# First norm from token rows in two channel halves, and expert outputs gathered by place, in a decoder step on one Trainium2 core

## The reference, cut to what matters

```python
def modulate(x, g, shift, scale):
    return rmsnorm(x, g) * (1 + scale) + shift
# per layer; the six parts are silu(c) @ ada_w + ada_b, 9 rows (prompt, 8 samples)
sh1, sc1, gt1, sh2, sc2, gt2 = adaln_params(c, ada_w[l], ada_b[l])
h = modulate(x, norm1_g[l], sh1, sc1)
z = h @ w_in[l]                       # 1536 columns: u | v | p
...                                   # gated chunk mixer and pooling mixer
x = x + gt1 * mix
h = modulate(x, norm2_g[l], sh2, sc2)
f = swiglu(h, ...)                    # layer 0: dense, 3584 wide
f = moe_swiglu(h, ...)                # layer 1: top 2 of 8 experts, each 3584 wide
x = x + gt2 * f
y = rmsnorm(x, final_g)               # after layer 1
```

## Time and profile before

| | |
|---|---|
| median of three runs | 1687.08 us (1686.13 to 1688.96) |
| profiled execution | 1686.33 us, span 1684.7 us |
| TensorE busy | 94% |
| vector, scalar engine busy | 71%, 57% |
| mean granted clock | 0.958 |
| moved by DMA | 492.97 MB, mean 293 GB/s |

### The profile page before, as it was taken

How to read it: one execution, slowest core, us unless ns; L and a number is a source line. 1 busy time by engine, 2 the same in 40 slices (tenths; PEclk the granted TensorE clock), 3 DMA queues, 4 the chain that set the end, 5 groups by cost and what they waited for, 6 DMA issues and landing times.

```text
span 1684.7 us, 22252 instructions
## 1 busy us (share of the span) xinstructions
PE 1585.7 (94%) x8280; PEld 1345.9 (80%) x8280; DVE 1188.7 (71%) x964; ACT 962.5 (57%) x717; POOL 63.4 (4%) x106
## 2 busy tenths in 40 slices
PE   6898999999996997899999999999999999999992
PEld 3675799999995767788888888888888888888881
DVE  2463454444445464588888889889888888888886
ACT  2432343333324333577777777777777777777774
POOL 2110000000000010100000000000000000000001
PEclk9896999999998978899999999999999999999996
DMA  9886474444432834499999999999999999999993
GB/s 324 283 289 242 146 255 150 149 149 149 150 124 101 299 114 162 162 377 374 372 389 376 382 380 382 387 373 374 393 371 368 394 379 374 390 379 376 379 378 106
DMA packets 245799, 492.97 MB, mean 293 GB/s; under 512 B 9839, under 2 KB 11031, under 8 KB 245750
## 3 DMA queue, kind: packets, MB, share of 16 engines
q1 hardware_dynamic: 236912, 471.10, 76.4%
q0 software_dynamic: 6160, 19.42, 3.4%
q10 hardware_dynamic: 2694, 1.99, 0.4%
HBM read 482.46 MB, written 10.25 MB: 292 GB/s over the span
## 4 chain that ended last, share of the span: by engine, by line
PE 92%; DVE 4%; DMA 2%; ACT 1%; issue 1%; POOL 0%; POOLq 0%; SPq 0%; ACTq 0%; DVEq 0%
PE ps L1393 19%; PE ps L1395 19%; PE ps L1394 19%; PE ps L1630 4%; PE ps L1631 4%; PE ps L1632 4%; PE ps L1412 2%; PE ps L1641 2%; PE ps L1642 2%; PE ps L1640 2%; PE ps L1441 2%; PE ps L1767 1%; PE ps L1524 1%; PE ps L1606 1%; PE ps L1525 1%; PE ps L1526 1%
## 5 line engine op out<-in xcount | busy, mean ns | idle before, releaser
L921 DVE TENSOR_TENSOR w_lo<-raw,w_hi 128x2048 fp32r<-128x2048 f32 x368 | 841.0, 2291 | 185.4 <-ACT w_hi L607 183.9
L607 ACT ACTIVATE w_hi<-raw 128x2048 fp32r<-128x2048 f32 x368 | 704.9, 1918 | 252.2 <-PE ps L1395 163.1
L1393 PE MATMUL ps<-w_hi,split 128*128 128x512 f32 x1392 | 549.3, 395 | 2.5 <-DVE split L1312 2.5
L1395 PE MATMUL ps<-w_hi,split 128*128 128x512 f32 x1392 | 543.7, 391 | 0.0
L1394 PE MATMUL ps<-w_lo,split 128*128 128x512 f32 x1392 | 543.4, 390 | 0.0
L1393 PEld LDWEIGHTS ps<-w_hi,split 128*128 128x128 f32 x1392 | 262.0, 188 | 61.3 <-issue 6.1
L1395 PEld LDWEIGHTS ps<-w_hi,split 128*128 128x128 f32 x1392 | 261.9, 188 | 55.1
L1394 PEld LDWEIGHTS ps<-w_lo,split 128*128 128x128 f32 x1392 | 262.0, 188 | 52.3
L1630 PE MATMUL ps<-split,w_hi 128*128 128x320 f32 x448 | 139.4, 311 | 1.1 <-DVE mod L962 1.1
L1631 PE MATMUL ps<-split,w_hi 128*128 128x320 f32 x448 | 139.2, 311 | 0.0
L1632 PE MATMUL ps<-split,w_lo 128*128 128x320 f32 x448 | 139.2, 311 | 0.0
(11 more groups left out here) (259 smaller groups left out, 1404.9 us busy)
## 6 DMA issues: line engine op xcount, KB each, us to landing
raw<-in_moe_w SPq DMA_DIRECT2D x338, 1024.0 KB, 7.1
raw<-in_ada_w SPq DMA_DIRECT2D x48, 1024.0 KB, 6.9
raw<-in_ffn_w SPq DMA_DIRECT2D x42, 1024.0 KB, 5.0
raw<-in_w_in SPq DMA_DIRECT2D x12, 1024.0 KB, 9.1
raw<-in_w_out SPq DMA_DIRECT2D x8, 1024.0 KB, 6.7
item_rows<-plain POOLq DMA_DIRECT2D x12, 512.0 KB, 7.4
plain<-in_x_prompt ACTq DMA_DIRECT2D x2, 512.0 KB, 8.4
tok_rows<-plain POOLq DMA_DIRECT2D x2, 512.0 KB, 3.3
```

What stands on the lines that cost most here:

```text
L607: a.activation(w_hi[:, (s0 + j) % SPL], raw[:, (u0 + j) % RAW], ACT.Copy).then_inc(hi_ready, 1)
L921: v.tensor_tensor(w_lo[:, (s0 + j) % SPL], raw[:, (u0 + j) % RAW], w_hi[:, (s0 + j) % SPL].bitcast(F32), ALU.subtract).then_inc(lo_ready, 1)
L1393: t_.matmul(out, a_hi, b_hi, start=first_, stop=False)
L1395: return t_.matmul(out, a_lo, b_hi, start=False, stop=last_)
```

## The change

1. **Order.** `FIRST_MOD` becomes shift 0, scale 0, shift 1, scale 1 by halves of the channels; the first w_in unit is loaded behind the first two blocks. The condition rows are loaded by SP ahead of the weights. TensorE does twelve products of a matrix of ones while it waits for them.
2. **First norm.** ACT squares the token rows with a row sum (`first_std`) and takes the root of three columns; DVE takes the reciprocals and scales a unit matrix by them (`diag`); TensorE multiplies ones by `diag`, so that each column of the result holds its token's factor, and DVE scales x from PSUM. The sum of squares over channels goes away. x is transposed in two halves, with block (0, 2) between them.
3. **Halves.** Gain, affine, high and low part are made for channels 0 to 511 from the first two blocks and for 512 to 1023 from the other two. The fold of the last block stands inside unit 0 of `project_in(0)`, behind two of its four slabs.
4. **Expert outputs.** The two places of a token and their gates are sorted, the smaller place first. ACT copies each item's output in two halves. POOL stores all items but the last; SP stores the last one in two halves. The rows of the smaller places are gathered, multiplied by gate and `gt2` and added to x behind POOL's and DVE's loops over the items; the rows of the larger places are gathered after the last store and take two operations. One more block of `item_rows` is set to zero in the FFN stage.

```diff
-FIRST_MOD = [(0, c) for c in range(4)]
+FIRST_MOD = [(0, 0), (0, 2), (0, 1), (0, 3)]
-PARTS = ([("ada", FIRST_MOD)] + mixer_parts(0) + ...
+PARTS = ([("ada", FIRST_MOD[0:2]), ("in", 0, 1), ("ada", FIRST_MOD[2:])] + mixer_parts(0)[1:] + ...
 @@ SP
+        sp.dma_start(crow[0:1, :], d['c_prompt']).then_inc(c_in, 16)
+        sp.dma_start(crow[1:ROWS, :], d['c_sample']).then_inc(c_in, 16)
+        load_ada(FIRST_MOD[0:2])
+        load_in(0, 0)
+        load_ada(FIRST_MOD[2:])
...
+        last_rows = d['item_rows'][bass.ts(n_items - 1, P), :]
+        for c, copied in enumerate((y_half, y_cp)):
+            sp.wait_ge(copied, n_items + c)
+            sp.dma_start(last_rows[:, c * B:(c + 1) * B], e_y[:, c * B:(c + 1) * B]).then_inc(y_last, 16)
 @@ POOL
-        with gp.Fori(0, n_items) as i:
+        with gp.Fori(0, n_items - 1) as i:
...
         gp.wait_ge(pos_int, 1)
         for b in range(NBLK):
+            fetch_outputs(b, 0, y0, y_early)
+        gp.wait_ge(y_last, 32)
+        for b in range(NBLK):
+            fetch_outputs(b, 1, y1, y_in)
 @@ ACT
+        def first_std():
+            act.wait_ge(x_in, 16 * N_X)
+            for b in range(NBLK):
+                n = BLK[b]
+                if b:
+                    act.wait_ge(row_sq, b)
+                a.activation(x_sq[0:n, 0:D], xtok[0:n, b, :], ACT.Square,
+                             accum_out=v_mv[0:n, b, 0:1]).then_inc(row_sq, 1)
+            act.wait_ge(row_sq, NBLK)
+            act.wait_ge(zeroed, 1)
+            a.activation(v_std[:, 0:2], v_mv[:, 0:2, 0], ACT.Sqrt, scale=1.0 / D, bias=eps[:])
+            a.activation(v_std[0:NS_TOK, 2:3], v_mv[0:NS_TOK, 2, 0:1], ACT.Sqrt, ...).then_inc(std_ready, 1)
...
         ada(*FIRST_MOD[0])
-        act.wait_ge(zeroed, 1)
-        norm_std(0, 0)
+        first_std()
         ada(*FIRST_MOD[1])
+        hi_to(S_IN[0] + 1)
+        ada(*FIRST_MOD[2])
+        first_affine(0)
         act.dma_start(gw_raw, ...)
-        ada(*FIRST_MOD[2])
         ada(*FIRST_MOD[3])
-        hi_to(S_IN[0] + 1)
-        norm_affine(0, 0)
+        first_affine(2)
...
+            act.wait_ge(split_used, i * N_FFN + (S_MOE + N_FFN - 1))
+            act.wait_ge(y_free, i + 1)
+            a.activation(e_y[:, 0:B], ps[:, 3, :], ACT.Copy).then_inc(y_half, 1)
             act.wait_ge(split_used, i * N_FFN + (S_MOE + N_FFN))
-            act.wait_ge(y_free, i + 1)
-            a.activation(e_y[:], ps[:, 3:5, :].rearrange("p a c -> p (a c)"), ACT.Copy).then_inc(y_cp, 1)
+            a.activation(e_y[:, B:D], ps[:, 4, :], ACT.Copy).then_inc(y_cp, 1)
 @@ DVE
+            if k == 3:                      # after the fourth copy of x
+                ve.wait_ge(std_ready, 1)
+                ...                         # reciprocals of three columns
+                for b in range(NBLK):
+                    ins = v.tensor_scalar(diag[0:n, b, :], ident[0:n, :], v_rstd[0:n, b:b + 1], None, ALU.mult)
+                ins.then_inc(diag_ready, 1)
...
+            if n == 0:
+                for half in range(2):
+                    for key in FIRST_MOD[2 * half:2 * half + 2]:
+                        ada_add(*key)
+                    first_gain(half)
+                    scale_pair(2 * half)
+                    scale_pair(2 * half + 1)
+                    if half == 0:
+                        lo_to(S_IN[l] + 1)
+                    lo_pair(2 * half)
+                    lo_pair(2 * half + 1)
+                return
...
+        for b in range(NBLK):               # behind the loop over the items
+            ve.wait_ge(y_early[b], 16)
+            step(v.scalar_tensor_tensor(out=y0[b][0:n], in0=y0[b][0:n], scalar=y_gate[0:n, 0, b:b + 1],
+                                        in1=(gt2p if b < 2 else gt2s)[0:n], op0=ALU.mult, op1=ALU.mult))
+            step(v.tensor_tensor(y0[b][0:n], y0[b][0:n], x_tok[0:n, b, :], ALU.add))
 @@ TensorE
+        for _ in range(N_WARM):             # 12
+            t_.matmul(ps[:, 3, 0:P], ones[:], ones[:], start=True, stop=True)
...
+        x_transpose(0)
+        ada(*FIRST_MOD[1])
         pe.wait_ge(prep_cp, 2)
+        ada_tr(*FIRST_MOD[0])
+        x_transpose(KB)
+        pe.wait_ge(diag_ready, 1)
+        for b in range(NBLK):
+            ins = t_.matmul(ps[:, 0, b * P:b * P + n], ones[0:n, :], diag[0:n, b, 0:n], start=True, stop=True)
+        ins.then_inc(ssum, 1)
+        ada_tr(*FIRST_MOD[1])
+        ada(*FIRST_MOD[2])
+        ada_tr(*FIRST_MOD[2])
+        ada(*FIRST_MOD[3])
 @@ TensorE, project_in
+                        if l == 0 and j == 0 and k == 2:
+                            ada_tr(*FIRST_MOD[3])
```

More of the change, by code:

```diff
@@ L347, in write_program @@
     y_free = sem("y_free")
+    y_half = sem("y_half")
+    y_last = sem("y_last")
+    y_early = [sem(f"y_early{b}") for b in range(NBLK)]
     y_in = [sem(f"y_in{b}") for b in range(NBLK)]
-    y_gate = sem("y_gate")
     y_sum = sem("y_sum")
@@ L549, in _ @@
                 step(g.memset(zero_rows, 0.0))
-                for e in range(E, NI):
+                for e in range(E - 1, NI):
                     gp.dma_start(d['item_rows'][e * P:(e + 1) * P, :], zero_rows).then_inc(zero_out, 16)
@@ L668, in norm_affine, with first_affine @@
                     a.activation(h_hi[:, 2 * b - 2:2 * b, 0:T], hf[:, 2 * b - 2:2 * b, :], ACT.Copy).then_inc(hhi, 1)
+        def first_affine(b0):
+            for b in range(b0, b0 + 3):
+                if b < b0 + 2:
+                    act.wait_ge(scaled, b + 1)
+                    for k in (2 * b, 2 * b + 1):
+                        a.activation(hf[:, k, 0:NP_TOK], hf[:, k, 0:NP_TOK], ACT.Identity,
+                                     scale=gain[:, 0, 0, k, 0:1], bias=mod[:, 0, k, 0:1]).then_inc(affine, 1)
+                if b > b0:
+                    act.wait_ge(affine, 2 * b)
+                    a.activation(h_hi[:, 2 * b - 2:2 * b, 0:T], hf[:, 2 * b - 2:2 * b, :], ACT.Copy).then_inc(hhi, 1)
         def project_in(l):
@@ L965, in ada_add, with first_gain @@
                             ALU.add).then_inc(mod_add, 1)
+        def first_gain(half):
+            ve.wait_ge(mod_add, BLOCK[0, 2 + half] + 1)
+            k = 4 * half
+            step(v.scalar_tensor_tensor(out=gain[:, 0, 0, k:k + 4], in0=mod[:, 0, KD + k:KD + k + 4, :], scalar=1.0,
+                                        in1=vec[:, 0, R_N1 + k:R_N1 + k + 4].unsqueeze(2).to_broadcast([P, 4, ROWS]),
+                                        op0=ALU.add, op1=ALU.mult))
         def ada_gain(l, which):
@@ L1307, in _ @@
         v.tensor_copy(table[:], tab[:]).then_inc(routed, 1)
+        v.tensor_tensor(later[:], pos[:, 0], pos[:, 1], ALU.is_gt)
+        v.tensor_tensor(place[:, 0], pos[:, 0], pos[:, 1], ALU.min)
+        step(v.tensor_tensor(place[:, 1], pos[:, 0], pos[:, 1], ALU.max))
+        v.tensor_copy(posi[:], place[:])
+        step(v.tensor_scalar(sooner[:], later[:], -1.0, 1.0, ALU.mult, ALU.add))
+        for j in range(2):
+            v.tensor_tensor(part[:, j, 0], gate[:, j], sooner[:], ALU.mult)
+            ins = v.tensor_tensor(part[:, j, 1], gate[:, 1 - j], later[:], ALU.mult)
+        step(ins)
+        v.tensor_tensor(y_gate[:], part[:, :, 0], part[:, :, 1], ALU.add).then_inc(pos_int, 1)
         def xs_split_lo(n):
@@ L1445, in _ @@
         ada(0, 0)
-        pe.wait_ge(x_in, 16 * N_X)
-        for k in range(KD):
-            if k >= 2:
-                pe.wait_ge(x_cp, k - 1)
-            for b in range(NBLK):
-                n = BLK[b]
-                ins = t_.transpose(ps[:, 2 + k % 2, b * P:b * P + n], xtok[0:n, b, k * P:(k + 1) * P],
-                                   ident[0:n, 0:n])
-            ins.then_inc(prep_tr, 1)
         pe.wait_ge(vec_in, 16 * N_VEC)
```

109 lines of the change are left out of this document (54 added, 55 removed).

## The result

The changed kernel takes 1671.69 us, median of 4 runs (1668.03 to 1673.99), against 1687.16 us in 4 runs of the kernel before beside it (1686.13 to 1688.96). The ratio is 0.9902, 95% interval 0.989 to 0.9914. The forecast was 1673.5.

What follows compares the result with a forecast made beforehand. The prediction saw no single engine bounding the front, TensorE pacing the experts, and a 32.6 us tail. From the profiled 1686.33 us it took 7.4 (tail) and 6.2 (front), then added 0.75 for the median: 1673.5, range 1668.5 to 1680.0.

Steps and rivals of the forecast that it cites:

- The tail: Last matmul to end: half copy, three late gathers and early vector work gain 7.4 us, bounds 5.5 and 8.5.
- the front: Start to unit 1: its first matmul at 56.0 instead of 62.3, 6.2 us gained, bounds 9.5 and 1.0.
- The last item: Early gathers beside the last expert item's weight loads fit the 12.2 us slack: 0, bounds 0 and +3 us.
- Item boundaries: Between expert items, two copies of 0.6 us for one of 1.02 cost nothing: 0, bounds -0.3 and +1.5.
- The front to unit 0: Input projection: first main matmul at 42.0 instead of 49.79, unit 0 ends at 50.3 instead of 58.77, at 2.4 GHz.
- Step (h): Behind unit 0: mask weights land at 52.5, 54.6 at the latest; unit 1 starts at 56.0 instead of 62.3.
- rival A: Front: mask weights or w_in 1 late, TensorE stands after unit 0, resumes at 1.2 GHz; 1677.7 to 1679.7 us, chance 0.18.
- The other branch of the step: Before unit 1: the split of w_in 1 is done at 56.0 and sets unit 1's start.
- The mixer: Behind the front: the mixer repeats its own waits and carries the front's gain on, 0 us of its own.
- rival C: Mixer: shifted phase leaves a stretch at 1.2 GHz, costing up to 12 us; 1691.7 if the front also fails; chance 0.10.

Runs made afterwards that it cites:

- Experiment 6: Changed kernel with the early gathers issued only after the last store, ahead of the three late ones: 1680.13 us, ratio 0.9951.
- experiment 10: Changed kernel with each early block of rows gathered twice during the last item, 2.56 MB instead of 1.28: 1677.14 us, ratio 0.993.
- experiment 5: Changed kernel with both halves of an item's last copy held back until the last down-projection unit is done: 1676.99 us, ratio 0.9933.
- Experiment 3: Changed kernel with the mask weights' load issued behind the first weight copy, ahead of the third modulation block: 1668.09 us, ratio 0.9887.
- Experiment 4: No warm-up products: in the changed kernel 1673.38 us; in the kernel with early mask load and early bias 1666.04 us.

## Why the prediction was right, and which terms were off

The tail was right by its mechanism. The total was right partly by luck, by terms that cancel: at the gelu of layer 0 the front is 4.8 us short of the forecast, and three other terms gave 3.6 more than they were booked at. In terms of the profiles, 13.6 was predicted (7.4 + 6.2) and 12.4 came.

- **The tail: 7.4 predicted, 8.2 measured, mechanism right.** The late half copy (0.60), the first landing (4.7) and the run of the vector engine came as written. The early work ended 9.1 us behind the last matmul (9.2 predicted). The first late gather was issued 3.5 us behind it and not 4.6, since the last half landed after 2.2 us (2.8 booked) and POOL came sooner behind that; the vector engine's early work hid this. What was 0.7 too long is the run behind it: 12.6 us were booked to the last scaling's end, and it took 11.9 (1657.10 to 1668.97), with one pause of 0.15. Experiment 6 shows that the fetch during the last item is worth 7.7 us, and experiment 10 that twice the bytes no longer fit there.
- **The last item: 0 predicted, 0 measured.** The slack of 12.2 us against 9.1 + 3.1 was called just enough; the trace has three waits of the scalar engine, 0.9 at most, that TensorE never sees. Doubling the bytes costs 4.3 us. 3 us of delay more for the second 1.28 MB, by the same arithmetic, is the right order: TensorE waited 2.3.
- **Item boundaries: 0 predicted, 1.4 measured.** The step looked at the scalar engine's total time and its idle time in a unit, and not at what stands behind the copy in its order: a weight copy and then a split that TensorE wants at once. What is copied behind the last matmul is 0.6 us instead of 1.03, and 1.2 in experiment 5, which takes the gain away with one moved wait (118.45, 118.64 and 118.70). The waits of the weight loads show it: seven of 0.3 us before, none after, seven of 0.4 in experiment 5.
- **The front to unit 0: a little better than predicted.** First main matmul 40.99 (42.0), end of unit 0 49.1 (50.3), at clock 1.00. The weight landed at 13.57 (14.6), and the second half of x took 2.25 (3.2). Both blocks beside it ran at the low clock, 3.57 and 3.62, where 3.25 was booked. The high level for unit 0 held.
- **Step (h), the mask weights: failed.** The forecast put the landing at 52.5, between 50 and 54.6. It was 54.0, the late end: issued 3 us sooner than I had it (39.4, not 42.4), but 14.6 us on its way, longer than the 12.2 of the earlier trace rows. The forecast had leaned on a queue that holds less once DMA has rested. DMA did rest (1 GB/s from 36 to 38 us), but it went to work again with SP's held-back weight units at the same moment (219 GB/s in 38 to 40, 402 in 40 to 42), and this load went among them. That put the wait of 4.9 us behind unit 0. The wait then had a second price that my sum did not count together with it, the low clock for transposes (3.0, not 1.6), ada block (3.57, not 1.93) and the first matmuls. Unit 1 started at 60.69, not 56.0: rival A at the front, with 1.2 GHz behind the landing as it said, though the landing, 54.0, lies short of the 55 from which A was to decide. The other branch of the step was too long as well: the split of w_in 1 was done at 54.1, not 56.0. Experiment 3 proves the step: earlier issue alone puts unit 1 at 53.36 and the gelu 6.0 us sooner. The Trainium skill (TensorE: Matmul & The Clock Gate, HAM oscillation) says that a wait between bursts drops the array to its low clock; here 4.9 us of standing did it (0.50 to 0.55 behind it), and so did 3.8 us ahead of the fold at 31.32 (1.00 from 24.0 to 27.5, 0.50 from 31.3 to 36.7), while the pauses of 0.6 and 0.7 us ahead of unit 0 did not.
- **The mixer: 0 predicted, 1.4 measured**, with its sign the opposite of rival C. The same work, from the first transposes of the mixer to the next fold, before and then after, shows it (busy PE, loads, DVE, ACT, POOL, then the clock):

```profile
114.87:132.15 17.28, 17.28 (x63) 13.12 (x62) 13.27 (x23) 7.00 (x6) 7.16 (x8) 0.60 0.80 274
```
```profile
113.45:129.25 15.80, 15.80 (x63) 12.04 (x62) 13.28 (x23) 7.00 (x6) 7.17 (x8) 0.68 0.80 265
```

  The same 63 matmuls, without a pause in either, take 15.80 us instead of 17.28, at a mean clock of 0.68, not 0.60. Rival C named the clock of the mixer as what could move, and it did, by about a tenth of its price. What sets the length of these low stretches is open. Experiment 4 shows another one, in layer 1, that is worth 4 us and differs between executions of the same code; whether the spread of 1668 to 1674 comes from it, no trace says.
- **By medians** the change gained 15.5, by profiles 12.4. The prediction went from the profiled execution to the median with 0.75; after, the median lies 2.3 *under* the profiled execution. So part of the closeness of 1671.7 to 1673.5 is this choice of execution.

## What to carry to other kernels

When a chain at the front is shortened, list every load whose issue stands behind a step of that chain in some engine's program order; a load moved to "after the step" still needs its time on the way, and that was 11.2 to 14.9 us for 512 KB in these runs. A wait for it costs twice, by itself and by the low clock behind it. In a stage that one engine paces, a copy at the end of an item is dear if the next unit's chain stands behind it: 0.4 us less of copy gave 0.19 us at each boundary, and only the waits of the weight loads showed it. At the end, fetch what is already complete while the last item computes, but count its bytes against the slack of the weight slots: 1.28 MB was free and 2.56 MB cost 4.3 us; and check that helpers put beside a vector engine that is busy 2.3 of every 2.73 us leave it its speed.

## What the runs showed of the hardware that was not expected

- The granted clock given for the first microseconds can be wrong. In the changed kernel the eight ada matmuls took 1.94 us at a clock given as 0.50; without warm-up products the same eight took 1.93 us, and the clock reads 1.00. Window of the changed kernel, then window and timeline of the one without warm-up products:

```profile
12.00:14.00 2.00, 0.90 (x8) 0.50 1.06 377
```
```profile
12.00:14.00 2.00, 0.85 (x8) 1.00 1.05 360
```
```profile
13.27 1.93 PE L1490 MATMUL ps<-raw,cT 128*32 128x512 f32 x8 [1.15 <-DMA raw<-in_ada_w]
```

  Eight matmuls in 1.93 us are 0.24 each, which is the low level (sixteen took 1.93 at 1.00). So there the duration tells the clock, and not the column. The Trainium skill (TensorE: Matmul & The Clock Gate, Seeing it yourself) warns that such events are unreliable; the trace agrees.
- Elementwise work on POOL is slow and unsteady: the multiplication of 128x1024 by a column took 3.3 and twice 7.0 us, the two-tensor ones 2.6 to 4.3, where the vector engine takes 1.28 us for the fused pair.
- A weight load of the front, w_in 2, landed 19.8 us after its issue, where the expert stage's take 7.0 to 8.1 by the median.
